# A two-layer hybrid decoder trunk: attention scores issued behind the transposes of the preceding batch of heads

## The reference

```python
for l in range(DEPTH):
    h = rms_norm(x, norm_mix[l])
    x = x + hybrid_mixer(h, w_in[l], w_out[l], ...)
    h = rms_norm(x, norm_ffn[l])
    x = x + peer_ffn(h, peer_query[l], ...)
return rms_norm(x, norm_final)
```

```python
logits = jnp.einsum('bnqhgd,bnkhd->bnhgqk', qb, kb) * (dh ** -0.5)
logits = jnp.where(valid, logits, NEG_BIG)
probs = jax.nn.softmax(jnp.concatenate([logits, sink], axis=-1), axis=-1)[..., :-1]
out = jnp.einsum('bnhgqk,bnkhd->bnqhgd', probs, vb)
```

## Time and profile before

| what | value |
|---|---|
| runs | 3627.41, 3619.2, 3610.1 us, median 3619.2 |
| profiled execution | 3624.84 us, its span 3622.6 us |
| mean granted TensorE clock | 0.958 of full |
| TensorE (PE) matmul busy | 79% of the span |
| VectorE (DVE) busy | 61% |
| ScalarE (ACT) busy | 21% |
| GpSimd (POOL) busy | 38% |
| attention batches, layer 0 | 189.9 to 289.4 us of the span |
| attention batches, layer 1 | 1987.6 to 2089.8 us |

### The profile page before, as it was taken

How to read it: one execution, slowest core, us unless ns; L and a number is a source line. 1 busy time by engine, 2 the same in 40 slices (tenths; PEclk the granted TensorE clock), 3 DMA queues, 4 the chain that set the end, 5 groups by cost and what they waited for, 6 DMA issues and landing times.

```text
span 3622.6 us, 31542 instructions
## 1 busy us (share of the span) xinstructions
PE 2871.8 (79%) x10443; PEld 1662.0 (46%) x10443; DVE 2196.6 (61%) x3080; ACT 760.8 (21%) x1189; POOL 1392.2 (38%) x1028
## 2 busy tenths in 40 slices
PE   7999938878787788777789999388777877787776
PEld 7887824433342343232388778234333423332322
DVE  6765576665656566655566655765656655665655
ACT  4344411111111111111143444011111111111111
POOL 0000046545545555544400000555545555555443
PEclk9999969999999999999999999699999999999999
DMA  5434579999999999999944344899999999999998
GB/s 190 142 127 150 197 284 408 414 418 413 416 419 414 404 419 419 415 416 415 420 145 141 127 165 161 338 411 417 414 412 411 419 421 408 415 416 418 413 419 362
DMA packets 239655, 1243.78 MB, mean 343 GB/s; under 512 B 24680, under 2 KB 33072, under 8 KB 107440
## 3 DMA queue, kind: packets, MB, share of 16 engines
q0 software_dynamic: 147456, 1073.81, 72.1%
q1 hardware_dynamic: 92080, 168.51, 13.6%
HBM read 1240.14 MB, written 2.10 MB: 343 GB/s over the span
## 4 chain that ended last, share of the span: by engine, by line
DMA 36%; PE 32%; DVE 17%; issue 8%; DVEq 3%; ACT 2%; POOL 2%; POOLq 0%; SPq 0%; ACTq 0%
DMA work<-in_peer_v_dram,idx_v 21%; PE PS L502 16%; DMA work<-in_peer_u_dram,idx_u 14%; PE PS L801 13%; DVE work L1702 6%; POOL work L1140 2%; DVE xs L1715 2%; DVE lo L1268 2%; DVEq L1379 1%; ACT hi L860 1%; DVE gain L1646 1%; DVE gain L1647 1%; ACT work L934 1%; DVE gain L1680 0%; DVE gain L1649 0%
## 5 line engine op out<-in xcount | busy, mean ns | idle before, releaser
L801 PE MATMUL PS<-work,diag 128*128 128x512 f32 x3968 | 1855.5, 615 | 640.0 <-DMA work<-in_peer_v_dram,idx_v 455.9
L1702 DVE CUSTOM_DVE_ANT_0 work<-work,hn 128x2048 f32<-128x2048 f32 x512 | 1164.3, 2291 | 851.2 <-DMA work<-in_peer_u_dram,idx_u 820.7
L801 PEld LDWEIGHTS PS<-work,diag 128*128 128x128 f32 x3968 | 739.6, 195 | 1726.0 <-issue 1302.8
L1140 POOL DMA_INDIRECT work<-in_peer_u_dram,idx_u x512 | 775.4, 1514 | 1501.2 <-DVEq L1686 941.6
L1140 POOL DMA_INDIRECT work<-in_peer_v_dram,idx_v x512 | 616.6, 1204 | 700.0 <-PE PS L801 565.4
L1069 ACT ACTIVATE diag<-cst,act_k 128x128 f32<-128x128 f32 x496 | 190.1, 398 | 1383.9 <-PE PS L801 1374.0
L502 PE MATMUL PS<-hT_hi,hi 128*128 128x256 f32 x1024 | 306.6, 299 | 43.8 <-DVE lo L1602 16.2
L502 PE MATMUL PS<-hT_lo,hi 128*128 128x256 f32 x1024 | 295.8, 289 | 0.0
L502 PE MATMUL PS<-hT_hi,lo 128*128 128x256 f32 x1024 | 295.7, 289 | 0.0
L502 PE MATMUL PS<-hi,hT_hi 128*128 128x512 f32 (+1 forms) x704 | 278.5, 396 | 9.9 <-ACT work L904 4.1
L502 PE MATMUL PS<-hi,hT_lo 128*128 128x512 f32 (+1 forms) x704 | 272.1, 386 | 0.0
(11 more groups left out here) (251 smaller groups left out, 1615.1 us busy)
## 6 DMA issues: line engine op xcount, KB each, us to landing
raw<-in_w_in_dram SPq DMA_DIRECT2D x40, 1024.0 KB, 5.0
gain<-in_w_in_dram SPq DMA_DIRECT2D x38, 1024.0 KB, 5.0
raw<-in_peer_query_dram SPq DMA_DIRECT2D x24, 1024.0 KB, 16.1
raw<-in_w_out_dram SPq DMA_DIRECT2D x16, 1024.0 KB, 5.1
gain<-in_w_out_dram SPq DMA_DIRECT2D x16, 1024.0 KB, 5.1
work<-in_peer_query_dram SPq DMA_DIRECT2D x8, 1024.0 KB, 7.4
work<-in_peer_u_dram,idx_u POOLq DMA_INDIRECT x512, 14.3
work<-in_peer_v_dram,idx_v POOLq DMA_INDIRECT x512, 14.0
```

The lines of the kernel that those rows point to most:

```text
L801: mm = pe.matmul(PS[:, j, :], diag[:, n % RING, :], vrow[n % RING][:, j * 512:(j + 1) * 512], start=(k == 0), stop=(k == (TOPK - 2 if last ...
L1140: pool.indirect_dma_start(out=dst, out_offset=None, in_=tables[table], in_offset=bass.IndirectOffsetOnAxis(ap=idx, axis=0)).then_inc(loade ...
L1702: dve.tensor_tensor_reduce(r, r, hn[:, b, :], 1.0, 0.0, ALU.mult, ALU.add, pre[:, b, k:k + 1]).then_inc(u_free.sem, 1)
```

## The change

scores(n+1) moves from behind attend(n) (after piece 26+2n) to right behind turn_probs(n) (after piece 25+2n). On VectorE soft(n+1) moves ahead of convolve(n-1) and take_attended(n), and since it now overwrites `probs` right behind the transposes, it also waits `probs_turned`. The due numbers of the splits sink by one, so a split comes where the piece two before it has just been multiplied. On ScalarE piece 27+2n is rounded between the exponentials and the copy of batch n, ahead of the wait for the transposes. And drain(6) comes behind batch 2 and no longer behind batch 3.

```diff
--- before.py
+++ after.py
@@ -673,12 +673,11 @@
                                                start=False, stop=True)
                     mm.then_inc(hgrn_out.sem, 1)
 
-                def batch_step(n):
+                def probs_step(n):
                     def go():
-                        if n > 0:
-                            attend(n - 1)
-                        if n < NBATCH:
-                            scores(n)
+                        turn_probs(n)
+                        if n + 1 < NBATCH:
+                            scores(n + 1)
                     return go
 
                 steps = {}
@@ -687,10 +686,10 @@
                     steps[LEVEL_STEP[i]] = lambda i=i: level(i)
                 steps[LEVEL_STEP[NL] + 1] = gate_turn
                 steps[22], steps[23] = turn_q, turn_k
-                for n in range(NBATCH + 1):
-                    steps[24 + 2 * n] = batch_step(n)
-                    if n < NBATCH:
-                        steps[25 + 2 * n] = lambda n=n: turn_probs(n)
+                steps[24] = lambda: scores(0)
+                for n in range(NBATCH):
+                    steps[25 + 2 * n] = probs_step(n)
+                    steps[26 + 2 * n] = lambda n=n: attend(n)
                 steps[37] = spread_m
                 steps[38] = lambda: m_scores(0)
                 steps[39] = lambda: m_scores(1)
@@ -934,6 +933,7 @@
                         a = act.activation(pr[:, i, :], pr[:, i, :], ACT.Exp, bias=nmx[:, b, h:h + 1], scale=DH ** -0.5,
                                            accum_out=rowsum[:, b, h:h + 1])
                     a.then_inc(exped.sem, 1)
+                    round_to(28 + 2 * n)
                     act.wait_ge(probs_turned.sem, probs_turned.upto(l, n + 1))
                     act.activation(probsT, bank(4, 2), ACT.Copy).then_inc(probs_taken.sem, 1)
 
@@ -966,8 +966,8 @@
                 drain(5)
                 batch_exps(1)
                 batch_exps(2)
+                drain(6)
                 batch_exps(3)
-                drain(6)
                 batch_exps(4)
                 drain(7)
                 batch_exps(5)
@@ -1457,8 +1457,11 @@
 
                     b, h0, nh = BATCHES[n]
                     hs = slice(h0, h0 + nh)
-                    split_to(27 + 2 * n)
+                    split_to(26 + 2 * n)
                     dve.wait_ge(scored.sem, scored.upto(l, n + 1))
+                    if n > 0:
+
+                        dve.wait_ge(probs_turned.sem, probs_turned.upto(l, n))
                     m = const("window")[:, 0:2 * P] if b == 1 else const("window")[:, P:2 * P]
                     pr = probs.rearrange("p (h s) -> p h s", h=nh)
                     for r in range(2):
@@ -1478,7 +1481,7 @@
                 def take_probs(n):
                     b, h0, nh = BATCHES[n]
                     hs = slice(h0, h0 + nh)
-                    split_to(28 + 2 * n)
+                    split_to(27 + 2 * n)
                     dve.wait_ge(exped.sem, exped.upto(l, n + 1))
                     dve.tensor_tensor(rinv[:, b, hs], rowsum[:, b, hs], esink[:, b, hs], ALU.add)
                     dve.drain()
@@ -1487,7 +1490,7 @@
 
                 def take_attended(n):
                     b, h0, nh = BATCHES[n]
-                    split_to(29 + 2 * n)
+                    split_to(28 + 2 * n)
                     dve.wait_ge(attended.sem, attended.upto(l, n + 1))
                     dve.tensor_tensor(hn[:, b, h0 * DH:(h0 + nh) * DH].rearrange("p (h d) -> p h d", h=nh),
                                       PS[:, 4, 0:nh * DH].rearrange("p (h d) -> p h d", h=nh),
@@ -1511,11 +1514,13 @@
                         d = dve.drain()
                     d.then_inc(conved.sem, 1)
 
+                soft(0)
                 for n in range(NBATCH):
-                    soft(n)
+                    take_probs(n)
+                    if n + 1 < NBATCH:
+                        soft(n + 1)
                     if 1 <= n < 5:
                         convolve(n - 1)
-                    take_probs(n)
                     take_attended(n)
```

## The result

| | before | changed |
|---|---|---|
| runs beside each other | 6, 3610.1 to 3627.4 us | 6, 3593.6 to 3600.3 us |
| median | 3619.4 us | 3599.35 us |
| ratio | | 0.994, 95% interval 0.9924 to 0.9956 |
| profiled execution, its span | 3624.84, 3622.6 us | 3598.67, 3596.9 us |
| mean granted clock | 0.958 | 0.956 |

The change takes off 20 us, 0.55%; forecast were 19.7. The interval of the ratio runs from 0.44 to 0.76% faster, so there is a gain, but the 0.5% from which the prediction counts a difference lies inside it.

The account below looks back on a forecast made before the run. TensorE was taken to bound the projection stage. 14.4 us idle, 4.7 clock and 0.6 refill sum to 19.7 us, taking the median 3619.2 to 3599.5 us; range 3586 to 3614.

Parts of the forecast that it names:

- TensorE bounds the stage: Projection stage, attention windows: TensorE's busy time equals the window where it never waits, so any excess goes into the time.
- The floors: Six attention windows per layer: TensorE's work alone is 15.58, 15.31 and four times 15.03 us; 19.7 us lie above.
- Idle, 14.4 us: Attention windows, both layers: waits of the transposes, piece 32 and piece 37, 6.7 and 7.65 us, all go.
- The waits of batch 0: First batch, scores not moved: soft(0) no longer behind piece 26's split wins about 1.2 us against waits of 0.9 and 1.2.
- drain(6): Ahead of piece 32: copy and drain a batch sooner remove the 2.0 us wait in each layer, with 0.25 us refill.
- Clock, 4.7 us: Three windows with granted clock 0.91: their slow matmuls behind long waits go, winning 4.7 us; bounds 0 and 6.3 us.
- The rival that kept them, 15.0 us: Attention windows: clock stays low where it was, only idle goes; 15.0 us gained, 3604.2 us; chance 0.20.
- The fourth slow piece: Behind spread_m in layer 0: 7.21 us without a wait, against 5.58 in layer 1; taken as staying.
- Costed at nothing: New probs_turned wait, VectorE's reordered work and early rounding: nothing on the path; 4.4 us spare for the chain, 2.5 on VectorE.
- VectorE doesn't become the bound: Rival, attention windows: soft and convolution ahead of the even split make even pieces wait, leaving 8 us gain, 3611; chance 0.10.
- The slower rival: ScalarE ahead of the copy: rounding waits for its load, about 60 us lost less 19.7, giving 3660 us; chance 0.03.
- Nothing opened behind the stage: Rival, turn of the mixed tiles: an idle of the same size opens there, no change, 3619 us; chance 0.04.

Follow-up runs that it names:

- the large dose: Changed kernel with eleven extra ScalarE passes, some 8.2 us, ahead of the exponentials of batches 1 to 5: 3626.7 us, one run.
- the kernel of three dues: Changed kernel with three due numbers of splits shifted on VectorE (pieces 21 and 45 among those moved): 3597.6 us, median of 5, ratio 0.9945.

## Why the prediction was right

**TensorE bounds the stage, and an idle there is time lost.** Right. 21.8 us came out of the windows and 20 us out of the median; the large dose put 29.8 us in and 27 us came out at the end. The reading of the earlier trace rows at its head was not: the two dips of the clock row are slices 6 and 26 of 40, 453 to 543 and 2264 to 2355 us, behind the projection stages and not where the layers begin. Nothing was worked out from it.

**The floors.** The term that was mis-sized: 19.7 us were summed, 21.8 measured, 1.0 us more in each layer. I took batch 2, 15.03 us with idle 0.00, as free of waits. It wasn't. Here are the last exponential and the transposes of batch 2 of layer 0 in the kernel before,

```profile
228.43 0.19 ACT L934 ACTIVATION_READ_ACCUMULATOR work<-work,nmx 128x1 f32 x1
```
```profile
228.30 0.39 PE L502 MATMUL PS<-hi,hT_lo 128*128 128x512 f32 x1
228.67 0.55 PE L612 MATMUL PS<-cst,work 128*128 128x128 f32 x3
```

and the transposes in the changed one:

```profile
228.00 0.39 PE L502 MATMUL PS<-hi,hT_lo 128*128 128x512 f32 x1
228.23 1.03 PE L612 MATMUL PS<-cst,work 128*128 128x128 f32 x8
```

From the start of the piece's last matmul to the transposes it is 0.37 us before and 0.23 now. The exponentials were through at 228.62, the transposes began at 228.67: they waited 0.14 us, hidden under the modelled end of the matmul, so no view called it idle. In the kernel before, the transposes of all twelve batches start 0.05 to 0.06 us behind the last exponential, so none was free of the chain. A window such as batch 2's is 14.88 to 14.91 us now and was 15.03; by an estimate from this, twelve windows give about 1.7 of the 2.1 us.

**Idle, 14.4 us.** Right, each one: the transposes' waits, piece 32's and piece 37's are gone. The waits of batch 0, where only half a split was won, are gone in both layers too, but with 0.2 us to spare.

**drain(6).** Right that both waits of 2.0 us go. But the parts share this otherwise than the prediction had it: the new order with the drain left in place already halves them (0.94 us is left), and the drain's new place in the old order takes them away but opens a wait of 0.75 us.

**Clock, 4.7 us.** Right in the changed kernel: the three slow stretches in the windows are gone. The rival that kept them, 15.0 us, is out: no window without a wait has one, and the large dose, which puts waits back, brings four back. The Trainium skill ("TensorE: Matmul & The Clock Gate", "Why this matters for your kernels") warns of longer idle gaps only. These traces don't bear that out: 5 of 9 idles of 2.0 to 2.5 us in the windows were followed by the low clock, and 12 of 18 of 1.76 us in another place (below). The fourth slow piece was right to leave out of the sum.

**Costed at nothing.** All held, with more room than worked out. The exponentials are through 5.7 to 6.9 us before the transposes, where 4.4 us were forecast: I had started soft at the latest that the scores could end (3.9 us), and it starts at the end of the split (2.5 us behind the piece in batch 4: 245.60 and 243.12). With the rounding counted 2.5 us were forecast, and 4.0 are there in batch 4 (it ends at 254.07, the transposes start at 258.03); the 5.0 us of ScalarE's idle hold the transposes as well. The even split ends at 255.3 and piece 34 starts at 260.1: 4.8 us spare, forecast 2.5. There the prediction left out that transposes and scores, 2.05 us, still stand ahead of the even piece. The loads were a little worse than forecast: ScalarE waits for even pieces three times in layer 0, 3.0 us together and 1.9 at most, against "0.5 us at the worst". Nothing of it reaches TensorE.

**The other rivals.** VectorE doesn't become the bound: soft could even stand behind the convolution. The slower rival, a rounding held by its load, didn't come: odd pieces wait at most 0.4 us, and taking the rounding away costs 1.6 us per layer, so it helps. Nothing opened behind the stage: piece 37 to the mixed tiles is 51.4 us in both layers, and the wait of 2.75 us in their turn is there before and after.

**The number.** 3599.5 forecast and 3599.35 measured is closer than the method deserves. The windows gave 2 us more than the sum, and the scatter of the rest took it back. The lower end of the range, 3586, doesn't follow from its terms either: 3619.2 less 21.3 and 9 is 3589.

## What to carry to other kernels

When an engine that bounds a stage waits for a chain over other engines, try to move the head of the chain up, to the first place where its buffers are free: here one group of matmuls issued a piece earlier, with the work behind it in step, turned a shortage of up to 2 us into a reserve of 5.7 or more (batch 0, whose head couldn't move, has 0.2). Shortening a link of the chain instead wasn't tried. Price such a wait from windows of equal work, and check that the one taken as the floor isn't on the edge itself. And expect prices to depend on the order around them: behind batch 3 the same 1 us drain went with a wait of 2.0 us in the old order and 0.9 us in the new, and behind batch 2 with one of 0.75 us in the old order and none in the new.

## What the runs showed of the hardware

**Idle and the granted clock.** Over the eleven profiles here, in the six windows: of 11 idles of 2.0 us or more 7 were followed, in the same or the next piece, by matmuls at the lower level, 1.2 GHz (0.43 us from start to start in place of 0.23). Of 7 idles of 1.4 to 1.8 us one was. Of the shorter ones none was, nor was any of 72 windows without a wait. Length doesn't decide alone, though: the wait of 1.76 us ahead of piece 21, the same in nine profiles and both layers, was followed by slow pieces in 12 of 18 cases. In the six others piece 22 waited 0.53 us instead, for the split that the slow piece had covered. The idle of 2.54 us at piece 22, in the kernel of three dues, was followed by the lower level in both layers. But of 18 idles of 2.75 us in the turn of the mixed tiles (the same nine profiles) only 5 came with it before the next wait; in 2 it came behind that wait, and in 11 not at all. So an idle of TensorE of about 2 us can cost another 1.5 to 1.6 us (in the windows) or 0.7 us (at pieces 21 and 22) or nothing, and neither its length nor its place alone says which.

**A slow piece without an idle.** The piece behind spread_m (8 matmuls on 4 rows of the array, and 4 tiny transposes, 2.1 us in which TensorE counts as busy) took 7.2 us rather than 5.6 in 10 of 22 cases, in either layer, with and without waits ahead. What in that stretch brings it on wasn't tried.
